# Other pacing for the second layer's image part beside the third and fourth tile of expert rows

## The chip, the cores and the metric

The kernel runs on one core of a Trainium2 chip. The metric is the device time of one execution in microseconds (us). Five engines work side by side: TensorE (PE, matrix products), VectorE (DVE), ScalarE (ACT), GpSimd (POOL, which here issues the gathers of expert rows) and SyncE (SP, which here issues the weight loads). They are tied together by semaphores only: an engine works through its own list in order, and an instruction that waits holds up everything behind it in that list.

## The reference, cut to what matters

Three layers of one network run one after another over 256 image tokens (x) and, in the first layer, 256 context tokens (ctx). Two layers are of the first kind, one is of a second kind. All is fp32, the model width is 1024. A layer of the first kind is a token mixer and then a retrieval over 16384 experts:

```
for l in range(DEPTH):                       # DEPTH = 2
    h  = _modulate(x,   norm1_g[l], m_x[0], m_x[1])
    hc = _modulate(ctx, norm1_g[l], m_c[0], m_c[1])
    mix_x, _ = _token_mix(h, lp, ang, kv_c)  # attention, Fourier mix, pooling, three sigmoid gates
    x = x + m_x[2] * mix_x
    h2 = _modulate(x, norm2_g[l], m_x[3], m_x[4])
    x = x + m_x[5] * _peer(h2, ...)
    if not last: the same for ctx

def _token_mix(h, lp, ang, kv_ctx):
    z = h @ lp["w_in"]
    cq, ckv, kr, zf, zp, zg = jnp.split(z, SPLITS, axis=-1)
    ...
    g = sigmoid(zg + lp["b_gate"])
    return (g_a * y_a + g_b * y_b + g_c * y_c) @ lp["w_out"], (k, v)

def _peer(...):   # for each token the 128 best experts (8 heads x 16)
    a   = einsum("tkd,td->tk", peer_down[ee], hh)
    act = gg * gelu(a)
    return einsum("tk,tkd->td", act, peer_up[ee])
```

With depth 2, the image part of the second layer's mixer (norm, projections `h @ w_in`, the attention vectors, Fourier and pooling mix, two of its three gated branches) needs the image tokens only, and these are finished when the first layer's experts of the two image tiles are done. The context tiles' experts still run then.

## The kernel before, in words

The tokens of the first layer form four tiles of 128: tiles 0 and 1 are x, tiles 2 and 3 are ctx. The expert stage (`gather`) goes through 4 x 128 = 512 rows; a row is the same place k of the 128 chosen experts for all 128 tokens of a tile. For row s, POOL fetches 128 vectors of `peer_down` (512 KB) and, for row s-18 (`LAG`), 128 vectors of `peer_up` (another 512 KB). DVE multiplies the down vectors with the token vectors and sums (a 128x1024 instruction, L1360). ACT applies the activation for 16 rows at a time and makes from each weight column a 128x128 diagonal matrix (L2809). PE multiplies the diagonal with the up vectors and adds into PSUM. In tiles 0 and 2 PE does both halves of the 1024 columns (L2150 and L2152); in tiles 1 and 3 PE does the first half alone and DVE the second half (L1387). An fp32 product is two instructions in the trace, so a row of the third tile is four 128x512 instructions on PE and a row of the fourth tile two. There are five buffers for down vectors and five for up vectors (`ND`, `NU`, L83): POOL fetches into one when the row that used it has been consumed (L3042 and `freed`, L3066).

Beside the rows runs other work, as a list of small units. `weave` (L216) sets the order on every engine. After each row the allowance `owed` grows by the rate (1.15 in this stage, `RATE0`), and as long as it is 1.0 or more one more unit is put behind the row, and its cost is taken off. `at` (L255) gives the units of a stage their cost; without it a unit costs 1.0. A unit that says `("after", n)` sets `hold`: no further unit is put in before row n. Each engine emits its own part of a unit at the same place of its own list.

The list beside the first layer's rows is `ctx_then_x` (L691): the queries of the image tiles, the whole context part of the first layer's mixer, the context tiles' queries and expert choice, and last `x_mix` (L671), the image part of the second layer's mixer. `x_mix` is, in order:

- `modulate`: norm and transposes of the image tokens, 6 units of cost 1.0
- `tok_major` twice (L1810 on PE): `h @ w_in` for 512 and then 416 columns, two units each; a unit is eight products of 128x512 or 128x416
- `qkvs` (L342): latent norms, query, key and value products, rotation, transposes, for two tiles, 12 units
- `spread` (L1929): Fourier and pooling mix, 9 units
- `gates` (L1971): for each of 8 column blocks of 128 a weight load by SP, then three gate products (eight products of 128x256 each) and two branch products (two of 128x256 each): 40 units

SP loads each weight block into one of two slots here, and a load waits until PE has read the slot's earlier content (L3082). After the 512 rows, 18 more steps finish the up vectors; then a fence ends the stage, and the image part's rest (`x_second`) follows on its own.

Of the kernel before, what the change touches and what calls it, by code (L numbers as in the profile page):

```python
# [85 lines left out]
NEXT = 128  # L86
# [47 lines left out]
class Walk:  # L134
# [447 lines left out]
    def main(self):  # L582

        K, A, NB = self.K, self.K.A, self.K.NB
        GR, BG, BCR, GR2 = K.GR, K.BG, K.BCR, K.GR2
        area = lambda *ranges: Mem(K.arena, *ranges)
        zrow = lambda t: K.H2[:, t, 0:928]
        zpair = lambda who: K.H2[:, 2 * who:2 * who + 2, 0:928]
        tables, gelu, gelu2 = (A["peer_down"], A["peer_up"]), ACT.Gelu_apprx_tanh, ACT.Gelu

        def temps(mem):
            return dict(qt=mem(768), kt=mem(768), kvt=mem(1024), junk=mem(256), rt=mem(3, 128), CQ=mem(2, 128), CK=mem(128))
# [11 lines left out]
        HTc, KTc, VVc = m0(8, 256), m0(8, 256), m0(2, 512)  # L604
        after_c = BG + 5120
        QT, AFP = m0(8, 256), m0(8, 256)
        AT, FT, PL = AFP[:, 0:4, :], AFP[:, 4:6, :], AFP[:, 6:8, :]
# [60 lines left out]
        MX, ga = K.arena[:, T0:T0 + 2048].rearrange("p (k n) -> p k n", n=256), K.arena[:, T0 + 2048:T0 + 4096].rearrange("p (k n) -> p k n", n=256)  # L668
        L1E = T0 + 4096

        def x_mix():  # L671
            yield ("after", 2 * NEXT + 6)
            self.modulate_rows(1, A["norm1_g"][1], 0, 0)
            yield ("after", 2 * NEXT + LAG + 2)
            self.folded(2)
            self.fence()
            yield from self.at(1.0, self.modulate(1, A["norm1_g"][1], 0, 0, HTc))
            self.fence()
            for c0, n in ((0, 512), (512, 416)):
                yield from self.at(1.8, self.tok_major(1, c0, n, lambda i: K.H2[:, i, c0:c0 + n], (HTc,)))  # L680
            self.fence()
            self.small_weights(1)
            tm = temps(area((T0, NB)))
            yield from self.at(1.4, self.qkvs(1, tm, [(t, zrow(t), QT, KTc, VVc) for t in (0, 1)]))
            self.fence()
            yield from self.spread(1, PL, FT, zpair(0), MX.rearrange("p (f c) n -> p f c n", c=2)[:, 0:2, :, :], MX[0:64, 4:8, :])
            self.fence()
            mem = area((L1E, NB))
            yield from self.at(1.6, self.gates(1, {1: FT, 2: PL}, MX, [mem(256) for _ in range(3)] + [ga], mem(256), HTc))

        def ctx_then_x(queries):  # L691
            yield from ctx_mix(queries)
            yield from x_mix()
# [2759 lines left out]
```

## Time and profile before

| | |
|---|---|
| median of 3 runs | 4397.4 us (4389.34 to 4398.44) |
| profiled execution | 4398.4 us, span 4396.6 us |
| PE busy | 3386.3 us, 77% |
| DVE busy | 2579.1 us, 59% |
| POOL busy | 2034.0 us, 46% |
| ACT busy | 815.1 us, 19% |
| moved by DMA | 1330.31 MB, mean 303 GB/s |

The page cuts the span into 40 slices of 110 us. In each line a digit is a share in tenths; `PEclk` is the clock that the chip granted TensorE, `DMA` the mean busy share of the 16 DMA engines. The first layer's expert rows run from about 452 us to 2072 us (slices 5 to 19), the second layer's from about 2300 us, the third's from about 3640 us. Between them the DMA engines rest while PE works alone. Two levels of the granted clock occur, 1.2 and 2.4 GHz; the tables show their mean over a stretch as a share of the higher one, so 0.50 is the lower level throughout.

### The profile page before, as it was taken

The page shows a single profiled execution, that of the slowest core. Times are in us where ns is not written, and L with a number is a line of the kernel's source. Part 1 is how long each engine was busy: PE and PEld are TensorE (multiplying, and loading weights), DVE is VectorE, ACT ScalarE, POOL GpSimd, SP SyncE. Part 2 cuts the span into 40 slices and gives each one's busy share as a digit, 9 for nine tenths or more (in the row PEclk, how much of TensorE's full clock was granted, in tenths as well). Part 3 has the DMA queues.
Part 4 walks back from the last instruction along what each step waited for, and adds up shares of the span by engine and source line. Part 5 has one row for each costly group of instructions (what it writes and reads, how often), then busy time and mean ns, then how long its engine had stood idle before and what let it go on. Part 6 is the DMA issues. An engine that isn't in the chain of part 4 may idle for free.

```text
span 4396.6 us, 35895 instructions
## 1 busy us (share of the span) xinstructions
PE 3386.3 (77%) x11238; PEld 1726.4 (39%) x11238; DVE 2579.1 (59%) x5454; ACT 815.1 (19%) x1924; POOL 2034.0 (46%) x2148
## 2 busy tenths in 40 slices
PE   6889786888768789866687866676878887876666
PEld 2357442455334246511254422221366654422111
DVE  1412767566776844776346674667563347684776
ACT  1311111222111121211221111111231111111111
POOL 0200566656555645666116665566100005676665
PEclk9999899999879899955898988775989998999556
DMA  6663998999999989999849999999500039999999
GB/s 226 227 239 131 343 372 317 365 371 409 400 363 340 343 307 367 402 368 370 303 155 358 341 358 405 357 404 379 181 1 1 1 112 343 342 350 368 373 372 340
DMA packets 380787, 1330.31 MB, mean 303 GB/s; under 512 B 39500, under 2 KB 44876, under 8 KB 377016
## 3 DMA queue, kind: packets, MB, share of 16 engines
q0 software_dynamic: 313344, 1141.10, 69.2%
q1 hardware_dynamic: 61104, 164.18, 10.1%
q10 hardware_dynamic: 6152, 22.74, 1.4%
q8 instruction: 93, 1.52, 0.1%
q14 instruction: 94, 0.77, 0.0%
HBM read 1326.69 MB, written 1.17 MB: 302 GB/s over the span
## 4 chain that ended last, share of the span: by engine, by line
PE 31%; DVE 21%; DMA 16%; issue 13%; POOL 12%; another core or an unknown queue 5%; ACT 3%; DVEq 0%; ACTq 0%; POOLq 0%
PE ps L1700 30%; POOL arena L3074 11%; DVE arena L905 7%; DMA arena<-in_peer_up,arena 7%; DVE arena L892 5%; DMA arena<-in_peer_down,arena 4%; ACT arena L2461 2%; DMA arena<-in_peer_u,arena 2%; PE ps L1706 1%; DVE arena L1297 1%; DVE arena L1286 1%; DVE arena L1281 1%; DVE arena L1276 1%; DVE arena L913 1%
## 5 line engine op out<-in xcount | busy, mean ns | idle before, releaser
L1700 PE MATMUL ps<-arena 128*128 128x512 f32 (+8 forms) x10500 | 3282.6, 493 | 870.5 <-DMA arena<-in_peer_up,arena 239.3
L1700 PEld LDWEIGHTS ps<-arena 128*128 128x128 f32 (+4 forms) x10500 | 1633.5, 198 | 2446.7 <-issue 1928.0
L905 DVE SCALAR_TENSOR_TENSOR arena<-arena,ps 128x1024 f32<-128x1024 f32 x1024 | 1238.8, 1216 | 541.7 <-DMA arena<-in_peer_down,arena 269.2
L3074 POOL DMA_INDIRECT arena<-in_peer_down,arena x768 | 744.1, 969 | 667.8 <-DVE arena L909 270.0
L3074 POOL DMA_INDIRECT arena<-in_peer_up,arena x768 | 734.4, 956 | 566.0 <-PE ps L1700 295.2
L2461 ACT ACTIVATE arena<-arena 128x128 f32<-128x128 f32 (+5 forms) x1242 | 446.3, 386 | 1945.7 <-PE ps L1700 586.8
L3074 POOL DMA_INDIRECT arena<-in_peer_u,arena x256 | 245.7, 960 | 645.2 <-DVE arena L909 537.8
L905 DVE SCALAR_TENSOR_TENSOR ps<-arena,ps 128x512 f32<-128x512 f32 x508 | 383.3, 754 | 136.2 <-DMA arena<-in_peer_up,arena 73.4
L2461 ACT ACTIVATE arena<-ps 128x512 f32<-128x512 f32 (+4 forms) x349 | 191.0, 547 | 1145.2 <-PE ps L1700 630.8
L3074 POOL DMA_INDIRECT arena<-in_peer_v,arena x256 | 243.6, 952 | 153.4 <-issue 69.7
L892 DVE TENSOR_TENSOR arena<-ps,arena 128x512 f32<-128x512 f32 (+3 forms) x192 | 131.2, 684 | 265.0 <-PE ps L1700 220.6
L892 DVE TENSOR_TENSOR arena<-arena 128x512 f32<-128x512 f32 (+8 forms) x398 | 246.7, 620 | 66.9 <-ACT arena L2461 41.3
L1706 PE MATMUL ps<-arena 128*128 128x128 f32 (+2 forms) x738 | 129.6, 314 | 133.7 <-DVE arena L892 69.5
L892 DVE TENSOR_TENSOR arena<-arena,ps 128x256 f32<-128x256 f32 (+1 forms) x134 | 73.0, 545 | 229.5 <-PE ps L1700 194.0
L1706 PEld LDWEIGHTS ps<-arena 128*128 128x128 f32 (+2 forms) x738 | 97.4, 157 | 216.6 <-issue 113.9
L909 DVE COPY arena<-ps 128x512 f32<-128x512 f32 (+5 forms) x69 | 39.6, 574 | 202.2 <-PE ps L1700 149.6
L2461 ACT ACTIVATE arena<-ps,arena 128x256 f32<-128x256 f32 (+2 forms) x140 | 71.0, 507 | 415.5 <-PE ps L1700 257.8
L2461 ACT ACT_TABLE_LOAD x79 | 101.4, 1283 | 64.5 <-DVE arena L892 29.7
L1276 DVE MAX8 arena<-ps 128x8 f32<-128x128 f32 x128 | 28.6, 287 | 133.6 <-PE ps L1700 70.4
L3020 POOL DMA_DIRECT2D arena<-in_w_mod x40 | 30.5, 763 | 133.3 <-PE ps L1700 70.5
L905 DVE DVE_READ_ACCUMULATOR arena<-arena,ps 128x1 f32 x1024 | 84.2, 82 | 0.0
L913 DVE TENSOR_REDUCE arena<-ps 128x1 f32<-128x512 f32 (+2 forms) x50 | 30.3, 606 | 73.1 <-PE ps L1700 65.6
(34 smaller groups left out, 560.5 us busy)
## 6 DMA issues: line engine op xcount, KB each, us to landing
arena<-in_w_mod POOLq DMA_DIRECT2D x40, 1024.0 KB, 6.5
arena<-in_gate_blocks SPq DMA_DIRECT2D x16, 2048.0 KB, 7.8
arena<-in_w_in SPq DMA_DIRECT2D x14, 2048.0 KB, 7.8
arena<-in_w_pq SPq DMA_DIRECT2D x13, 2048.0 KB, 16.0
arena<-in_ada_w POOLq DMA_DIRECT2D x24, 1024.0 KB, 7.9
arena<-in_w_out SPq DMA_DIRECT2D x8, 2048.0 KB, 8.0
arena<-in_gate_blocks SPq DMA_DIRECT2D x8, 1792.0 KB
arena<-mod_scratch ACTq DMA_DIRECT2D x26, 512.0 KB
```

Source lines behind the costliest of these rows:

```text
L892: self.e.tensor_tensor(o, a, b, op).then_inc(*(inc or self.inc(self.S.vec)))
L905: self.e.scalar_tensor_tensor(o, a, s, b, op0, op1, accum_out=accum).then_inc(*(inc or self.inc(self.S.vec)))
L909: self.e.tensor_copy(o, a).then_inc(*(inc or self.inc(self.S.vec)))
L913: self.e.tensor_reduce(o, a, AX, op).then_inc(*(inc or self.inc(self.S.vec)))
L1276: e.max(v[j][:, 0:8], src[j]).then_inc(*self.inc(S.vec))
L1281: e.max_index(ix[j][:, 0:8], v[j][:, 0:8], src[j]).then_inc(*self.inc(S.vec))
L1286: e.match_replace(tmp[j], v[j][:, 0:8], src[j], NEG).then_inc(*self.inc(S.vec))
L1297: e.max_index(ix[j][:, 8:16], v[j][:, 8:16], tmp[j]).then_inc(*(self.drain(b) if last else self.inc(S.vec)))
L1700: return self.e.matmul(o, l, r, start=start, stop=stop)
L1706: ins = self.e.transpose(o, x, self.K.ident)
L2461: self.e.activation(o, i, f, bias=bias, scale=scale, accum_out=accum).then_inc(*(inc or self.inc(self.S.act)))
L3074: self.e.indirect_dma_start(out=o, out_offset=None, in_=table, in_offset=bass.IndirectOffsetOnAxis(ap=idx.bitcast(U32), axis=0)).then_inc( ...
```

## The change

Four numbers in the list beside the rows. The two projection stages cost 6.0 a unit where they cost 1.8, `qkvs` costs 2.8 where it cost 1.4, `spread` costs 2.8 where it cost 1.0, and a hold at row 384 (3 x `NEXT`) is put ahead of the gates, whose own cost stays 1.6. No instruction of the computation is added or removed.

```diff
             for c0, n in ((0, 512), (512, 416)):
-                yield from self.at(1.8, self.tok_major(1, c0, n, lambda i: K.H2[:, i, c0:c0 + n], (HTc,)))
+                yield from self.at(6.0, self.tok_major(1, c0, n, lambda i: K.H2[:, i, c0:c0 + n], (HTc,)))
             self.fence()
             self.small_weights(1)
             tm = temps(area((T0, NB)))
-            yield from self.at(1.4, self.qkvs(1, tm, [(t, zrow(t), QT, KTc, VVc) for t in (0, 1)]))
+            yield from self.at(2.8, self.qkvs(1, tm, [(t, zrow(t), QT, KTc, VVc) for t in (0, 1)]))
             self.fence()
-            yield from self.spread(1, PL, FT, zpair(0), MX.rearrange("p (f c) n -> p f c n", c=2)[:, 0:2, :, :], MX[0:64, 4:8, :])
+            yield from self.at(2.8, self.spread(1, PL, FT, zpair(0), MX.rearrange("p (f c) n -> p f c n", c=2)[:, 0:2, :, :], MX[0:64, 4:8, :]))
             self.fence()
+            yield ("after", 3 * NEXT)
             mem = area((L1E, NB))
             yield from self.at(1.6, self.gates(1, {1: FT, 2: PL}, MX, [mem(256) for _ in range(3)] + [ga], mem(256), HTc))
```

PE's list at the second projection block, before. The 128x416 products are this block's two units, the 128x128 transposes begin `qkvs`; the 128x512 products between them are up products of the third tile, two to a row, save eight in the first group that are the first block's last unit.

```order
L1700 MATMUL ps<-arena 128x512 x24
L1700 MATMUL ps<-arena 128x416 x8
L1700 MATMUL ps<-arena 128x512 x2
L1700 MATMUL ps<-arena 128x416 x8
L1700 MATMUL ps<-arena 128x512 x4
L1706 MATMUL ps<-arena 128x128 x2
L1700 MATMUL ps<-arena 128x512 x2
L1706 MATMUL ps<-arena 128x128
```

The same place of the changed kernel (its lines from 688 on are one higher):

```order
L1701 MATMUL ps<-arena 128x512 x38
L1701 MATMUL ps<-arena 128x416 x8
L1701 MATMUL ps<-arena 128x512 x10
L1701 MATMUL ps<-arena 128x416 x8
L1701 MATMUL ps<-arena 128x512 x10
L1707 MATMUL ps<-arena 128x128 x2
L1701 MATMUL ps<-arena 128x512 x6
L1707 MATMUL ps<-arena 128x128
```

Between two projection units stood one row's up products and now stand five rows'; between two units of `qkvs` stood one row's and now two or three.

PE's list where the gates begin, before: eight 128x256 are a gate product, two are a branch product.

```order
L1700 MATMUL ps<-arena 64x256 x2
L1700 MATMUL ps<-arena 128x512 x2
L1700 MATMUL ps<-arena 64x256 x4
L1700 MATMUL ps<-arena 128x512 x2
L1700 MATMUL ps<-arena 128x256 x8
L1700 MATMUL ps<-arena 128x512 x2
L1700 MATMUL ps<-arena 128x256 x8
L1700 MATMUL ps<-arena 128x512 x4
L1700 MATMUL ps<-arena 128x256 x2
```

And now:

```order
L1701 MATMUL ps<-arena 64x256 x2
L1701 MATMUL ps<-arena 128x512 x2
L1701 MATMUL ps<-arena 64x256 x4
L1701 MATMUL ps<-arena 128x512 x3
L1701 MATMUL ps<-arena 128x256 x8
L1701 MATMUL ps<-arena 128x512 x2
L1701 MATMUL ps<-arena 128x256 x8
L1701 MATMUL ps<-arena 128x512
L1701 MATMUL ps<-arena 128x256 x2
```

The gates moved from rows of the third tile (two 128x512 products each) to rows of the fourth (one each): where one row or two lay between two units, that was two or four products and is now one or two.

## Rows read from the trace of the kernel before

**Rows 1.** The page's slices: granted clock, DMA share, GB/s.

```profile
PEclk9999899999879899955898988775989998999556
DMA  6663998999999989999849999999500039999999
GB/s 226 227 239 131 343 372 317 365 371 409 400 363 340 343 307 367 402 368 370 303 155 358 341 358 405 357 404 379 181 1 1 1 112 343 342 350 368 373 372 340
```

**Rows 2.** Windows of the first layer's last rows, all engines.

```profile
core 0: us, PE busy (x) PEld busy (x) DVE busy (x) ACT busy (x) POOL busy (x), PEclk, DMA share, GB/s
1519.00:1561.00 42.00, 29.91 (x69) 13.13 (x68) 25.39 (x46) 12.11 (x27) 21.60 (x23) 0.82 0.92 339
1561.00:1605.00 44.00, 40.66 (x105) 19.10 (x105) 13.95 (x31) 10.04 (x27) 17.81 (x19) 1.00 0.79 278
1605.00:1640.00 35.00, 29.84 (x95) 14.59 (x94) 25.44 (x64) 9.47 (x25) 20.40 (x22) 0.95 0.93 325
1640.00:1704.00 64.00, 62.52 (x215) 37.69 (x214) 22.75 (x45) 16.07 (x38) 32.25 (x35) 1.00 0.91 334
1704.00:1849.00 145.00, 135.41 (x488) 90.80 (x486) 90.23 (x155) 31.95 (x78) 86.29 (x92) 1.00 1.01 399
1849.00:2072.00 223.00, 155.79 (x159) 38.74 (x160) 158.37 (x245) 32.65 (x85) 147.12 (x158) 0.54 0.98 372
```

**Rows 3.** The same windows for DVE's row instructions alone (line L905).

```profile
core 0: us, DVE busy (x), PEclk, DMA share, GB/s
1519.00:1561.00 42.00, 18.45 (x28) 0.82 0.92 339
1561.00:1605.00 44.00, 9.66 (x17) 1.00 0.79 278
1605.00:1640.00 35.00, 14.24 (x23) 0.95 0.93 325
1640.00:1704.00 64.00, 18.88 (x34) 1.00 0.91 334
1704.00:1849.00 145.00, 78.75 (x126) 1.00 1.01 399
1849.00:2072.00 223.00, 158.06 (x240) 0.54 0.98 372
```

**Rows 4.** Chain that ended last, 1555 to 1710 us, its longest pieces: start, us.

```profile
1554.95 32.28 PE ps L1700 x81
1596.46 7.76 PE ps L1700 x20
1618.74 11.18 PE ps L1700 x28
1637.46 25.79 PE ps L1700 x83
1666.96 19.40 PE ps L1700 x68
1687.19 23.15 PE ps L1700 x81
```

**Rows 5.** Timeline of DVE, then POOL: start, us, instruction, idle before it.

```profile
1579.94 0.59 DVE L909 COPY arena<-ps 128x416 f32<-128x416 f32 x1 [15.25 <-PE ps L1700]
1572.85 0.94 POOL L3074 DMA_INDIRECT arena<-in_peer_up,arena  x1 [5.65 <-PE ps L1700]
```

**Rows 6.** Timeline of PE: a third-tile row, and one projection block with rows.

```profile
1615.34 1.89 PE L1700 MATMUL ps<-arena 128*128 128x512 f32 x4
1560.81 29.84 PE L1700 MATMUL ps<-arena 128*128 128x512 f32 x75
```

**Rows 7.** Groups by shape, 1561 to 1849 us: xcount, busy us, mean ns, idle before.

```profile
L1700 PE MATMUL ps<-arena 128*128 128x256 f32 x480 | 111.3, 379 | 1.4 <-DVE arena L921 1.4
L2461 ACT ACT_TABLE_LOAD x11 | 14.1, 1283 | 9.6 <-PE ps L1700 8.8
L1700 PE MATMUL ps<-arena 128*128 128x416 f32 x32 | 11.5, 512 | 0.0
L1700 PE MATMUL ps<-arena 128*128 128x384 f32 x16 | 5.5, 485 | 0.0
L1706 PE MATMUL ps<-arena 128*96 128x128 f32 x32 | 4.6, 288 | 3.6 <-issue 3.6
```

**Rows 8.** Groups by shape, 1849 to 2072 us, rows with nothing beside them.

```profile
L1700 PE MATMUL ps<-arena 128*128 128x512 f32 x159 | 156.6, 1086 | 67.7 <-DMA arena<-in_peer_up,arena 41.1 <-issue 25.4 <-ACT arena L2461 1.2
L905 DVE SCALAR_TENSOR_TENSOR arena<-arena,ps 128x1024 f32<-128x1024 f32 x80 | 97.7, 1221 | 53.2 <-DMA arena<-in_peer_down,arena 34.1 <-issue 19.1
```

**Rows 9.** All of the first layer's rows: DVE line L905, one window.

```profile
453.00:2072.00 1619.00, 797.83 (x1273) 0.87 0.97 364
```

**Rows 10.** The page's DMA issues: the second layer's gate blocks, KB each.

```profile
arena<-in_gate_blocks SPq DMA_DIRECT2D x8, 1792.0 KB
```

## The prediction, made before the changed kernel had run

> **What bounds the kernel now.** I read the page's slices first [rows 1]. Where expert rows run the DMA digit is nearly always 9 (90% or more), so how fast 1 MB a row comes in sets the time. It dips to 8 in the fifteenth slice, 1539 to 1649 us, which is where the diff works. So I cut that part into windows [rows 2] and counted rows in each by DVE's own row instructions [rows 3]: two for a row of the third tile (the product and the read of its sum), three for one of the fourth.
>
> From 1849 to 2072 us the rows have nothing beside them: 240/3 = 80 rows in 223 us, 2.79 us a row, DMA share 0.98, 372 GB/s, and both PE and DVE wait mostly for the gathers [rows 8]. That is the DMA's pace. From 1561 to 1605 us there are 17/2 = 8.5 rows in 44 us, 5.2 us a row; DMA share 0.79, PE busy 40.66 of 44 at full clock. From 1605 to 1640: 11.5 rows, 3.0 each, DMA 0.93. From 1640 to 1704: 17 rows, 3.8 each, DMA 0.91, PE busy 62.52 of 64. From 1704 to 1849: the third tile's last 18 rows of down products take 36 of the 126 instructions and the other 90 are 30 rows, so 48 rows, 3.02 each, DMA 1.01 at 399 GB/s. In all 8.5+11.5+17+48+80 = 165 rows in 511 us.
>
> The chain says what the slow windows wait for [rows 4]: one piece of 32.28 us on PE, then 25.79, 19.40 and 23.15, with little between. Meanwhile DVE sits 15.25 us before one copy of a projection's result, with row products queued behind it, and POOL sits 5.65 us until PE frees an up buffer [rows 5]. So PE is the bound there, and the DMA engines lose 0.21 x 44 + 0.07 x 35 + 0.09 x 64 = 9.2 + 2.5 + 5.8 = 17.5 us.
>
> **Where the units stand now.** Counting the allowance through the list (1.15 a row), the preceding work ends at row 341 in both kernels, norm at 342 to 346, the first projection unit at 347. Before, the other three stand at 349, 351, 352; `qkvs` at 354 to 367; `spread` 368 to 376; gates 376 to 430; rows 431 to 530 are bare. Now the projections stand at 347, 353, 358, 363; `qkvs` 368 to 395; `spread` 397 to 417; gates 420 to 475; rows 476 to 530 are bare. The hold at 384 decides nothing, because the new costs reach row 417 first. All fits before the last row, so nothing is pushed behind the stage; the last row is still about 37 + 18 steps away.
>
> **The sum.** PE's needs at full clock: a third-tile row 1.89 us standing alone and 4 x 0.40 = 1.6 in a dense run (29.84 us for 75 instructions) [rows 6], I count 1.89; a projection unit 16 x 29.84/75 = 6.4 us [rows 6] or 11.5/2 = 5.8 [rows 7]; the whole of `qkvs` about 5.5 + 4.6 [rows 7] + eight 128x512 at 0.40 = 3.2 + small transposes, 15 us; gates 448 of the 480 instructions of 128x256, 448/480 x 111.3 = 104 us [rows 7]. A fourth-tile row is half of 1.89, 0.95.
>
> 1. Rows 348 to 368 (20, with three projection units): PE 20 x 1.89 + 18 = 56 us, 2.8 a row; DMA wants 2.79. Both near the limit and in lumps: a unit of 6 us behind one row and none behind the next four. Bounds: 2.8, and 3.95, the 79 us of 1561 to 1640 us over its 20 rows. I take 3.2, since the nearest window with units as thin beside third-tile rows ran at 3.0 [rows 2, 3] and the lumps come on top: 64 us.
> 2. Rows 368 to 401 (33, `qkvs` at half its density and two units of `spread`): PE 62 + 16 = 78 us, 2.4 a row. Bounds 2.79 and 3.4 (window of 1519 to 1561 us has 14 rows in 42 us = 3.0; the stage as a whole, 1619 us for 512 rows [rows 9], 3.16; PE at a mean clock of 0.7 would give 3.4). The window at twice the density of `qkvs` made 3.0, but it began with filled buffers, so I take 3.1: 102 us.
> 3. Rows 401 to 420 (19 light rows with `spread`): 2.8 to 3.1, taken 2.9: 55 us.
> 4. Rows 420 to 475 (55, all gates): PE 55 x 0.95 + 104 = 156 us, 2.84 a row. DMA: 55 x 1.049 MB plus eight blocks of 1.835 MB, of which one or two come in early (a slot is free after row 363, the other after `spread`), 57.7 + 12 = 69.7 MB [rows 10] at the 399 GB/s of the window that carries such blocks [rows 2]: 175 us, 3.2 a row. The gates were DMA-bound there before and stay so.
> 5. Rows 475 to 512 (37 bare) at 2.79: 103 us.
>
> Sum 64 + 102 + 55 + 175 + 103 = 499 against 511 us: 12 us less. Checks from outside: the bytes of 1561 to 2072 us are 44 x 278 + 35 x 325 + 64 x 334 + 145 x 399 + 223 x 372 = 186 MB. With 70 MB of it at 399 and the rest at 372 GB/s that is 175 + 312 = 487 us, so 24 us is all that this change can give back, and I expect half.
>
> Small edits on the way. ACT gets two more table loads, 81 against 79 in its list, because the activation of 16 rows falls between more of the square roots: 2 x 1.28 us [rows 7] on an engine busy 48 of 143 us from 1561 to 1704 and less beyond [rows 2]; hidden, at worst 2.6 us. The fences are the same in number and stand between units as before. SP's loads wait for slots that free later in rows; the first gate blocks still come before their products. The takeover of the token vectors at row 384 makes DVE wait for ACT; it now falls among `qkvs` units where it fell among gate units; either way ACT waits for PE there, and less if PE is not behind. After the stage nothing has moved.
>
> The profiled execution took 4398.4 us, 1.8 us beyond its span; 4398.4 - 12 = 4386.4 us. It lies 1.0 us above the median of the runs shown, within their 9 us spread. Forecast: 4386 us.
>
> **The rivals.**
>
> A. *Handovers, not PE's load, cost the time.* Every `qkvs` unit sends a value through ACT, DVE, PE and back while rows queue behind each wait. If spreading them only spreads the waits, rows 348 to 420 run at the stage's mean of 3.16 [rows 9]: 228 us where the forecast has 221, and up to 5 more if the 20 rows at the projections take 3.4. That leaves 0 to 5 us of the 12: about 4395, no change that can be told. For it: the fast part of the slow stretch still had DMA 0.93. Against it: the chain is PE by far [rows 4].
>
> B. *All of the DMA's idle time comes back.* 487 us by the bytes: 4374 us. Against it: no window with work beside third-tile rows reached 0.98 before.
>
> C. *PE's clock falls in the third tile, and the kernel gets slower.* Before, dense work kept the clock at 1.00 from 1561 to 1849 us; in the bare rows it is 0.54, and at 1519 to 1561, PE busy 30 of 42 us, it was 0.82 [rows 2]. Thinner work leaves PE pauses. A product instruction takes 1.086 us at the low level [rows 8], so a third-tile row 4.3 us. If the mean clock over rows 348 to 401 is 0.72, PE needs (56 + 78)/0.72 = 186 us there, where the forecast has 166, and pays waits of some 5 us on top: 4386 + 24 = 4410 us, slower by 12. It decides from a mean clock of about 0.78 down (172 us, and the waits, eat the 12 us gained). [...]
>
> The Trainium skill speaks for this rival: the page "TensorE: Matmul & The Clock Gate", section "HAM oscillation — how this bites in real kernels", advises to keep products together ahead of a DMA wait so that PE stays warm, the opposite of this change. The trace agrees that bare rows run at the low level; by that rule the time would be C's, by the rows the forecast's.
>
> D. *The change does not do what it says.* The gates do not begin with the fourth tile's first row but 36 rows later. That costs nothing by the count above, since 55 bare steps remain.
>
> **How the numbers follow.** I hold a change within 0.2% (9 us) for not told from none. Forecast, a gain of 6 to 18 us: 0.52. A: 0.24. B: 0.11. C: 0.13. D changes no time and has no chance of its own. Faster by more than 9 us: three quarters of the forecast's case and B, 0.39 + 0.11 = 0.50. Within 9 us: the rest of it and A, 0.13 + 0.24 = 0.37. Slower by more than 9 us: C, 0.13. The range runs from B's 4374 to 4402, which takes in A and the lighter cases of C and leaves under 2 in 10 out.
>
> **What would show it.** In the changed kernel's windows: row 348 to 368 should show a DMA share of 0.90 or more where 0.79 stood, and no DVE wait of 15 us before a projection copy. The clock over rows 348 to 401 should stay above 0.85. Gates should run at 3.2 us a row with a DMA share of 1.0, then about 37 bare rows at 2.8. The stage's last down product should come 12 us earlier. Wrong would be: clock below 0.78 (C); clock high, PE idle and still 3.2 us a row (A); gate rows above 3.3 us, which would mean that I sized the weight traffic too small.

## The result and the profile after

The changed kernel took 4367.35 us (median of 4 runs, 4356.71 to 4372.49) against 4393.37 us for the kernel before on the same chip: ratio 0.9926, 95% interval 0.9905 to 0.9947. It is faster by 26 us, where 12 were forecast and 4374 us was the lower end of the range. In a later comparison, of 7 runs against 27, the ratio was 0.9958, interval 0.9941 to 0.9975, which is 18 us. The two intervals overlap, so no closer number than 18 to 26 us can be given. The profiled execution took 4364.67 us, its span 4362.9 us.

The page's slices after, in the form of [rows 1]:

```profile
PEclk9999899999979899996899988866988998999556
DMA  6663998999999999999849999999400039999999
GB/s 228 227 237 130 338 363 320 375 356 409 401 362 355 343 378 352 392 410 375 298 159 369 333 365 392 372 405 374 157 1 1 1 113 338 352 350 372 379 369 346
```

The digit of the fifteenth slice, 8 before, is 9, and the rate of that slice is 378 GB/s where it was 307. Now the windows. The kernel after is cut where rows 336, 348, 368, 401, 420, 475 begin and row 511 ends, as DVE's row products show them (its lines from 688 on are one higher). First all engines, then DVE's row instructions alone:

```profile
core 0: us, PE busy (x) PEld busy (x) DVE busy (x) ACT busy (x) POOL busy (x), PEclk, DMA share, GB/s
1518.00:1552.00 34.00, 23.98 (x56) 10.05 (x55) 24.78 (x44) 12.43 (x28) 22.81 (x23) 0.82 0.99 375
1552.00:1617.00 65.00, 61.60 (x149) 27.84 (x148) 27.07 (x50) 14.18 (x33) 38.85 (x42) 0.99 0.93 363
1617.00:1720.00 103.00, 84.64 (x223) 39.33 (x221) 53.49 (x116) 24.50 (x64) 64.51 (x69) 0.94 0.96 364
1720.00:1775.00 55.00, 32.70 (x70) 13.09 (x71) 40.21 (x69) 8.93 (x25) 32.85 (x35) 0.79 0.96 362
1775.00:1946.00 171.00, 154.81 (x559) 104.29 (x558) 115.08 (x192) 36.82 (x91) 104.89 (x113) 0.99 1.02 405
1946.00:2043.00 97.00, 67.40 (x71) 16.73 (x70) 72.18 (x113) 15.50 (x38) 63.82 (x69) 0.57 0.99 378
```

```profile
1552.00:1617.00 65.00, 24.97 (x43) 0.99 0.93 363
1617.00:1720.00 103.00, 39.07 (x66) 0.94 0.96 364
```

The stretch from row 336 to the end of row 511, which the windows of both kernels cover from nearly the same microsecond (1518.9 and 1518.2), is the measure used below. It holds the same work in all kernels here, save where an edit below takes work out, adds some or moves other work into it. Before, its first profile and a second one (`before_again`), then after, first and second (`after_again`):

```profile
1519.00:2071.00 552.00, 453.66 (x1123) 213.63 (x1121) 335.18 (x580) 111.79 (x277) 324.77 (x347) 0.80 0.96 361
```

```profile
1523.00:2073.00 550.00, 455.28 (x1122) 214.21 (x1121) 335.04 (x579) 111.86 (x277) 324.34 (x347) 0.79 0.96 362
```

```profile
1518.00:2043.00 525.00, 425.12 (x1123) 211.33 (x1121) 332.81 (x580) 112.36 (x279) 327.73 (x347) 0.87 0.98 380
```

```profile
1527.00:2057.00 530.00, 430.85 (x1123) 215.82 (x1121) 330.87 (x580) 111.87 (x280) 328.54 (x348) 0.85 0.98 377
```

To a tenth: 552.5 and 550.8 us before, 525.1 and 530.2 after. The stretch lost 24 us on the mean of the two, 27.4 in the first pair; the rest of the first pair's 33.7 us lies in stages that the change does not touch. The bytes are the same, 552 x 361 and 525 x 380 GB/s are both 199 MB: the gain is the rate. Part of it is idle time of the DMA engines, 0.96 of 552 busy against 0.98 of 525. The other part is that the packets themselves took less: share x 16 engines / rate is the time that one engine spent on a KB, 0.96 x 16 / 361 = 42.5 ns before and 0.98 x 16 / 380 = 41.3 ns after.

The waits of [rows 5] are gone from the projections. DVE copies the first result of each projection block, and ACT the second. DVE's two copies after, in its timeline, with no idle time noted before either:

```profile
1558.62 0.69 DVE L910 COPY arena<-ps 128x512 f32<-128x512 f32 x1
1595.14 0.59 DVE L910 COPY arena<-ps 128x416 f32<-128x416 f32 x1
```

### The profile page after: what moved, and what is told of

It reads as the page before. It is cut to its first block, busy times and chain, and to the rows that moved or that the text cites. A ratio compares the mean times of both kernels' runs of the same rounds, so it can differ in the third digit from the quotient of the medians.

```text
span 4362.9 us, 35889 instructions
## 1 busy us (share of the span) xinstructions
PE 3358.4 (77%) x11238; PEld 1715.0 (39%) x11238; DVE 2577.2 (59%) x5454; ACT 816.5 (19%) x1926; POOL 2040.9 (47%) x2148
## 4 chain that ended last, share of the span: by engine, by line
PE 15%; DVE 10%; DMA 9%; issue 7%; POOL 5%; another core or an unknown queue 3%; ACT 2%; ACTq 0%; DVEq 0%; POOLq 0%
PE ps L1701 15%; POOL arena L3075 5%; DMA arena<-in_peer_up,arena 5%; DVE arena L893 3%; DVE arena L906 3%; DMA arena<-in_peer_v,arena 2%; ACT arena L2462 1%; DMA arena<-in_ada_w 1%; DMA arena<-in_peer_u,arena 1%; DMA arena<-in_peer_down,arena 1%; PE ps L1707 1%; DVE arena L914 1%; DVE arena L1287 1%; DVE arena L1282 0%
## 5 line engine op out<-in xcount | busy, mean ns | idle before, releaser
L1701 PE MATMUL ps<-arena 128*128 128x512 f32 (+9 forms) x10500 | 3254.6, 490 | 873.9 <-ACT arena L2462 231.9
L893 DVE TENSOR_TENSOR arena<-arena 128x512 f32<-128x512 f32 (+8 forms) x398 | 246.9, 620 | 72.1 <-ACT arena L2462 42.1
L893 DVE TENSOR_TENSOR arena<-arena,ps 128x256 f32<-128x256 f32 (+1 forms) x134 | 73.0, 545 | 222.7 <-PE ps L1701 171.2
```

Source lines behind the costliest of these rows:

```text
L893: self.e.tensor_tensor(o, a, b, op).then_inc(*(inc or self.inc(self.S.vec)))
L1701: return self.e.matmul(o, l, r, start=start, stop=stop)
```

## The experiments

All stretches are from row 336 to the end of row 511. "Row 368" is the time from row 336 to row 368: 121.1 and 119.9 us before, 98.5 and 99.8 after. In each fence of windows the first row is rows 336 to 368 and the second the whole stretch, rounded to whole microseconds.

**proj_only: the first number alone.**

```diff
-                yield from self.at(1.8, self.tok_major(
+                yield from self.at(6.0, self.tok_major(
```

> Only the first of the four numbers: the projection units cost 6.0, everything else as before. By the allowance the projections stand at rows 347 to 363 as in the changed kernel, the attention vectors at 368 to 382, spread to 390, gates 391 to 445, so most gates also leave the third tile. Measure: time from row 336 to the end of row 511, 552.5 us before and 525.1 us in the changed kernel. Theory P (PE's load beside third-tile rows is the bound, and any thinning gives back the DMA's idle time there): 24 to 28 us of the 27 come from here, because by row 368 the changed kernel is already 22.6 us ahead; stretch 525 to 529 us, device time 22 to 28 us under before. Theory H (handovers of the attention vectors cost, and their pacing matters as much): the dense attention vectors at rows 368 to 382 lose what they lost before, some 8 to 10 us; stretch 534 to 537 us.

```profile
1512.00:1610.00 98.00, 85.37 (x203) 38.37 (x202) 51.71 (x94) 25.35 (x61) 58.76 (x63) 0.91 0.94 362
1512.00:2046.00 534.00, 442.78 (x1123) 213.18 (x1122) 335.39 (x581) 113.68 (x280) 326.79 (x348) 0.82 0.97 374
```

534.2 us; device time ratio 0.9968 (0.9951 to 0.9984). All of the lead at row 368 is there (98.8), but 4 to 6 us of it are lost again by row 384 (158.3 against 152.0 and 154.6). The projections' pacing brings 17 to 18 us, most of the gain though not all of it. The number lies at the edge of H's range, and its loss stands where H put it: rows 368 to 401, with the attention vectors still dense, took 113.1 us where the changed kernel took 103.8 and 104.3. What of these last 4 to 9 us is handovers and what is PE's load, this run does not tell.

**vectors_only: the second and third number alone.**

```diff
-            yield from self.at(1.4, self.qkvs(
+            yield from self.at(2.8, self.qkvs(
-            yield from self.spread(1, PL, ...
+            yield from self.at(2.8, self.spread(1, PL, ...
```

> Only the second and third number: attention vectors and spread at 2.8, projections dense as before. Attention vectors at rows 354 to 380, spread to 402, gates 405 to 459. Theory P: the dense projections still cost their 14 to 20 us (rows 344 to 360), the rest is given back because the gates have left the third tile; stretch 540 to 543 us, device time 9 to 13 us under before. Theory H: the handovers were the loss, so most of it comes back; stretch 528 to 533 us.

```profile
1515.00:1625.00 110.00, 91.50 (x223) 41.37 (x222) 55.97 (x110) 27.08 (x71) 55.73 (x60) 0.90 0.88 323
1515.00:2053.00 538.00, 432.81 (x1122) 211.35 (x1120) 333.86 (x580) 109.74 (x278) 325.04 (x347) 0.85 0.97 371
```

538.1 us; ratio 0.9981 (0.9966 to 0.9995). Row 352 is where it was before (63.0 against 62.7), so the dense projections still cost; after them it gains 14 us, 11 of them by row 368 (110.5). P said 540 to 543, because the gates leave the third tile, and missed by 2 us; most of the gain stands where the attention vectors were thinned, and `gates_late` shows that the gates' move alone brings none. By the stretch the two parts alone make 31 to 33 us together, where both at once brought 24 to 27; by the device times they make 14 and 8 us, which is no more than the 18 to 26 of both. So whether they give back partly the same idle time is not shown.

**gates_late: old costs, the gates held to row 402.**

```diff
+            yield ("after", 3 * NEXT + LAG)
             mem = area((L1E, NB))
```

> Old costs throughout, but the gates held until row 402, the first whose up products DVE shares. Projections, attention vectors and spread dense at rows 347 to 376 as before, nothing beside rows 377 to 401, gates 402 to 451. Theory P: this removes the PE-bound gates beside third-tile rows (DMA idle 5.8 us from 1640 to 1704 us) and nothing of the projections'; stretch 544 to 548 us, 4 to 8 us under before. Theory G (that the gates beside third-tile rows were the main cost): 535 us or less. If the weight traffic alone were what counts, no change: 550 to 554 us.

```profile
1514.00:1635.00 121.00, 99.16 (x265) 46.37 (x264) 64.60 (x139) 31.64 (x79) 60.69 (x64) 0.92 0.87 311
1514.00:2066.00 552.00, 439.54 (x1124) 211.75 (x1123) 333.26 (x582) 109.51 (x277) 328.45 (x348) 0.85 0.95 362
```

551.7 us, no change; ratio 0.9993 (0.9975 to 1.0011). At row 384 it was 16 us ahead (169.6 against 185.2), and by row 475 all was gone (448.6 and 449.2). Rows 401 to 420 and 420 to 475 of this kernel, then of the kernel before:

```profile
1741.00:1804.00 63.00, 56.61 (x206) 40.02 (x204) 40.75 (x72) 12.28 (x30) 33.27 (x36) 0.95 0.92 350
1804.00:1963.00 159.00, 126.83 (x356) 68.60 (x356) 112.06 (x184) 29.54 (x76) 101.22 (x108) 0.85 1.01 394
```

```profile
1755.00:1817.00 62.00, 55.22 (x206) 38.14 (x206) 41.02 (x70) 15.77 (x36) 36.98 (x40) 1.00 1.01 397
1817.00:1968.00 151.00, 112.93 (x192) 40.06 (x190) 111.11 (x174) 24.51 (x64) 99.59 (x108) 0.65 0.99 382
```

The gates' 15 MB of weights had not come yet and came later, while the DMA share fell to 0.92 where the first gates met the change of tiles. So it is not the gates leaving the third tile that pays. P, which gave 544 to 548 us, missed here as G did; the number is that of the third case, no change. Why that share fell is open.

**thin_proj: the schedule of before, a quarter of the projections' products** (so later values differ from the reference).

```diff
+            ks = (0, 7) if l == 1 and n > 400 else range(8)
-            for k in range(8):
+            for k in ks:
```

> The kernel before with its schedule unchanged, but each projection unit of the second layer's image part does two of its eight products (the contraction is cut to a quarter, so the later values are not the reference's); loads, evictions, fences and all waits stay. It takes 24 of the 32 products, 18.6 us of PE at full clock, out of rows 347 to 352. Theory P: PE's load is the bound there, so the stretch shortens by 14 to 19 us, to 534 to 539 us. Theory H (the waits between engines bound it): less than 5 us, 548 us or more.

```profile
1517.00:1620.00 103.00, 82.54 (x220) 37.97 (x220) 65.81 (x141) 31.87 (x80) 62.00 (x64) 0.91 0.98 369
1517.00:2049.00 532.00, 432.81 (x1075) 203.96 (x1074) 335.76 (x581) 111.54 (x278) 327.31 (x347) 0.80 0.98 375
```

531.5 us, 19 to 21 less than before and 2.5 beyond P's range; ratio 0.9953 (0.9934 to 0.9971). All waits between engines stand where they stood in the lists, and taking 18.6 us of products out wins 18 to 19 us by row 368 (102.2). H, which gave less than 5 us, falls. The loss at the projections is PE's load.

**before_again and after_again** are the two kernels unchanged.

> The kernel before once more, to see how far the stretch from row 336 to the end of row 511 repeats from profile to profile. It was 552.5 us; the single-edit kernels that share its first rows agree within 0.5 us up to row 352 (62.7, 62.9, 63.0), so I expect 550 to 555 us.

> The changed kernel once more: stretch 523 to 528 us (525.1 before), and a tighter ratio of the device times; from the stretch alone 27 us or 0.6% are expected.

550.8 and 530.2 us. The second is 2 us outside its range: the stretch of the changed kernel repeats only to about 5 us, and differences smaller than that between the kernels below are none.

**gates_thin: the gates thinner still.**

```diff
-            yield from self.at(1.6, self.gates(1,
+            yield from self.at(2.2, self.gates(1,
```

> The changed kernel with the gates at 2.2 instead of 1.6 a unit, so that they fill rows 420 to 495 instead of 420 to 475 and 16 bare rows are left before row 512 instead of 37. Theory M (rows with weight loads among them move 400 to 410 GB/s, bare rows 365 to 377, because the DMA engines have more to choose from): rows 430 to 512 take 94 MB / 0.41 = 229 us where they took 236.8; stretch 517 to 521 us. Theory N (the mix does not matter, the bytes are only moved about): no change, 523 to 528 us.

```profile
1511.00:1613.00 102.00, 85.81 (x203) 37.99 (x202) 51.40 (x93) 26.55 (x61) 60.34 (x64) 0.92 0.93 355
1511.00:2039.00 528.00, 416.89 (x1123) 214.06 (x1121) 332.41 (x580) 112.79 (x281) 323.94 (x345) 0.89 0.98 378
```

528.2 us: theory M falls. Rows 430 to 512 took 241.2 us where M gave 229, and 236.8 and 240.3 in the changed kernel. Stretching the weight loads over more rows wins nothing. Ratio to before 0.9957 (0.9939 to 0.9975), that of `after_again` beside it 0.9958.

**warm_pe: PE kept busy in the bare rows of the kernel before.**

```diff
                 self.wait_ge(*there)
                 ...
+                if len(tiles) == 4 and s >= 440:
+                    spare = K.psum[:, 3584:4096]
+                    self.wait_ge(S.free[7], self.uses[7])
+                    self.mm(spare, K.ident, K.H2[:, 3, 0:512], True, True)
+                    self.mm(spare[:, 0:256], K.ident, K.H2[:, 3, 0:256], True, True)
```

> The kernel before, with two products whose result nobody reads (128x512 and 128x256, identity as weights) added on PE ahead of each row's up product from row 440 on, where rows are bare. [...] Theory W (bare rows are slow because PE at the low level frees the up buffers 1 us later): rows 448 to 512 fall from 2.84 to about 2.6 us each, 15 us in all. Theory M (the DMA's own rate for a lone queue is the bound): no change in those rows, within 3 us. Theory L (the added load itself counts): slower by the amount that PE goes over the row, seen as PE busy near 1.

Rows 448 to 512 of this kernel, then of the kernel before:

```profile
1890.00:2072.00 182.00, 153.15 (x384) 67.94 (x382) 126.45 (x195) 23.25 (x66) 117.75 (x126) 0.99 0.97 367
```

```profile
1890.00:2071.00 181.00, 126.09 (x127) 30.92 (x126) 125.67 (x194) 26.16 (x68) 118.79 (x128) 0.53 0.98 364
```

The clock went from 0.53 to 0.99 and the rows did not get faster. That does not yet make them the DMA's alone, because the run did not do what theory W needs, to free the up buffers earlier. The added products stand behind the wait for the up vectors (`there`), ahead of the row's own product. Here is one row of this kernel, with six instructions, and one of the kernel before, with two:

```profile
1951.28 2.39 PE L1700 MATMUL ps<-arena 128*128 128x512 f32 x6 [0.17 <-DMA arena<-in_peer_up,arena]
1903.63 2.04 PE L1700 MATMUL ps<-arena 128*128 128x512 f32 x2 [0.50 <-DMA arena<-in_peer_up,arena]
```

From the landing of the vectors to the free buffer PE took 2.4 us where it took 2.0, so what the clock gave the added work took away. W stays open by this run. Rows 440 to 448 moved 347 GB/s with the products added, where the two profiles before show 404 and 378. The kernel as a whole is slower, ratio 1.0033 (1.0017 to 1.0049), and the added products also stand in the 18 steps after the last down row: from the end of row 511 to the next stage's first row it took 240.3 us where before took 231.7, which is 9 of the 13 us between the medians.

**copy_late: DVE's copy one unit later, PE's list as before.**

```diff
+        late = l == 1 and n > 400
         for i in range(2 * len(HTs)):
             b = self.bank()
-            yield
-            if i % 2 == 0:
+            if late and i == 1:
+                yield
+                self.wait_ge(*self.full(first))
+                self.copy(dst(0), first.ap[:, 0:n], inc=self.drain(first))
+                continue
+            first = b
+            yield
+            if i % 2 == 0 and not late:
```

> The kernel before, with one thing moved: DVE's copy of a projection's first result stands one unit later in DVE's list for the second layer's image part (two rows further on). PE's list is the same. Theory P (PE's load beside third-tile rows): DVE's wait moves elsewhere, POOL still waits for PE to free up buffers, and by row 368 nothing is won: 119 to 121 us from row 336, stretch 549 to 553 us. Theory C (the copy that holds DVE's rows costs by itself): by row 348 it stands at 35 us as in the changed kernel, where the kernel before stands at 41 to 42, and by row 368 it is 6 us or more ahead; stretch 542 to 546 us.

POOL's waits for PE at the projections in this kernel:

```profile
1560.25 0.94 POOL L3081 DMA_INDIRECT arena<-in_peer_up,arena  x1 [6.74 <-PE ps L1707]
1570.57 0.94 POOL L3081 DMA_INDIRECT arena<-in_peer_up,arena  x1 [5.64 <-PE ps L1707]
```

551.4 us; ratio 0.9986 (0.9967 to 1.0004). By row 348 it stood at 35.2, 6 us ahead as theory C has it; by row 356 all but 1 us of that was gone, and at row 368 it had 119.6. POOL waited 5.64 us for PE where [rows 5] have 5.65. The 15.25 us that DVE sat before the copy were no cost of their own: had it not waited there, it would have waited for rows.

**proj_34: the changed kernel, projections at 3.4.**

```diff
-                yield from self.at(6.0, self.tok_major(
+                yield from self.at(3.4, self.tok_major(
```

> The changed kernel with the projections at 3.4 a unit instead of 6.0, so at rows 347, 350, 353 and 356, three up rows between two units where there were one or two before and are five now; the rest follows at the new pace, gates at 411 to 465. Theory P: three rows and a unit want 3 x 1.6 to 1.9 + 6.4 = 11 to 12 us of PE, 3.8 a row, still over the 2.6 to 2.8 of the DMA, but the debt is paid over the thin rows that follow, and five down and five up buffers cover little of it; row 368 at 103 to 108 us from row 336 (98.5 to 99.8 in the changed kernel, 120 to 121 before), stretch 529 to 534 us. If only the leaving of the dense place counted, it would stand at 99.

```profile
1527.00:1635.00 108.00, 92.94 (x220) 41.35 (x219) 54.98 (x103) 25.71 (x65) 60.04 (x62) 0.91 0.91 339
1527.00:2060.00 533.00, 434.35 (x1124) 214.58 (x1122) 334.70 (x580) 112.16 (x279) 327.86 (x346) 0.85 0.98 374
```

533.0 us and 107.2 at row 368, as PE's load has it: three rows' room for a unit gives about two thirds of the lead at row 368, five rows' room all. Ratio 0.9939 (0.9920 to 0.9958), not to be told from the changed kernel's.

**norm_thin and ctx_thin: the same idea one stage earlier, and beside the first tile.**

```diff
-            yield from self.at(1.0, self.modulate(1, ...
+            yield from self.at(2.6, self.modulate(1, ...
```

> The changed kernel with the norm's six units at 2.6 instead of 1.0, one per 2.3 rows; everything behind moves by eight rows, gates end at row 483. In the changed kernel rows 344 to 352 still show a DMA share of 0.79. Theory P: the four units of transposes (0.6 us each on PE) and the DVE products of the norm (1.2 to 1.3 us, five of them) come as a lump; thinned, 2 to 4 us come back, stretch 522 to 526 us against 525.1 and 530.2. Rival: the loss there is the chain of the norm itself (square, mean, root), which spacing does not shorten: no change, 525 to 531 us.

```diff
-            yield from self.at(1.4, self.qkvs(0, ...
+            yield from self.at(2.2, self.qkvs(0, ...
-            yield from self.at(0.97, self.attend(2, ...
+            yield from self.at(1.15, self.attend(2, ...
```

> The changed kernel with the same idea applied to the first layer's context part, beside the first tile's rows (PE does both halves of the up products there too): attention vectors at 2.2 instead of 1.4 and attention at 1.15 instead of 0.97 a unit; all that follows moves ten rows on, the gates of the second layer end at row 485. Rows 96 to 144 ran at a DMA share of 0.85 to 1.0 and 307 to 393 GB/s. Theory P: 4 to 8 us come back there, measured from row 96 to row 224, and the stretch from 336 is not comparable since other work stands in it; device time 4 to 8 us under the changed kernel's. Rival: these rows wait for the softmax's handovers (row maximum on DVE, exponential on ACT), not for PE's load, and spacing wins less than 3 us.

norm_thin stood at 195.0 us at row 401, 7 to 9 ahead of the changed kernel, and ended at 528.3, level with it and outside P's 522 to 526. ctx_thin took 418.7 us from row 96 to row 224 where the changed kernel took 427.6 and 434.5 and the kernel before 427.2 and 427.6. The 13 other profiles, which hold the same work in these rows, lie between 423.4 and 434.7, so some 5 us are won there. Its row 511 ended at 2052.0 us of the span where the changed kernel's ended at 2043.3 and 2056.9: won early, not there at the end. Ratios 0.9916 (0.9888 to 0.9943) and 0.9926 (0.9898 to 0.9953), of four runs each. Both intervals overlap those of the changed kernel, so no version here is shown to beat it.

## Why the prediction was wrong, step by step

The mechanism was right: PE was the bound beside the third tile's rows (`thin_proj`), thinning gave the DMA engines most of their idle time there back, and the clock stayed high (0.99 and 0.94, not under 0.78), so rival C did not come. The size was off, and two terms of the sum did it. Rows 336 to 348, which the sum left out as unchanged, gave 6 to 8 us, and the last 37 rows, put at 103 us, took 97 and 96. Together they are the 12 us that the forecast lacked. The terms of the sum, with both profiles of the changed kernel:

| rows | forecast | after, after_again | before, before_again |
|---|---|---|---|
| 336 to 348 | not in the sum | 34.2, 35.4 | 42.3, 41.0 |
| 348 to 368 | 64 | 64.3, 64.4 | 78.8, 78.9 |
| 368 to 401 | 102 | 103.8, 104.3 | 114.6, 114.2 |
| 401 to 420 | 55 | 54.7, 54.7 | 62.4, 62.4 |
| 420 to 475 | 175 | 171.2, 175.6 | 151.1, 150.9 |
| 475 to 512 | 103 | 96.9, 95.8 | 103.3, 103.4 |

1. *The sum began at row 348.* The forecast held everything before as unchanged, since the first unit stands at row 347 in both kernels. But the copy of its result stands in DVE's list at the next unit's place, two rows on before and six now, and DVE's rows queue behind it. The window lost 6 to 8 us. `copy_late` and `proj_only` both show 35 us there, and so does `thin_proj` (35.3), where the copy stands at its old place but PE's unit before it is short. By itself the later copy is worth nothing, as `copy_late` shows; together with PE's relief it stays.
2. *Bare rows at 2.79 us.* The last 37 rows took 2.6 each. The mean of 2.79 came from a window of 80 rows [rows 3] and was applied to a piece of 37 right behind the gates. In both kernels the first 18 rows behind the last gate ran faster than the others, and only then fell back to 2.7 to 2.9 us each: before, rows 430 to 448 took 46.2 us, 2.57 each; after, rows 475 to 493 took 45.2 and 42.1 us, 2.5 and 2.3 each. In the short piece they weigh twice as much: 6 to 7 us. These rows and the bare ones that follow, before, then after, then `after_again`:

```profile
1843.00:1890.00 47.00, 34.31 (x47) 9.73 (x45) 37.17 (x59) 9.52 (x24) 31.28 (x34) 0.67 1.02 406
1890.00:1968.00 78.00, 54.52 (x55) 13.31 (x54) 53.35 (x83) 11.33 (x30) 51.27 (x56) 0.52 0.97 359
1946.00:1991.00 45.00, 31.54 (x34) 8.11 (x34) 35.37 (x57) 8.02 (x19) 30.48 (x33) 0.58 0.99 383
1991.00:2043.00 52.00, 35.86 (x38) 8.62 (x36) 36.81 (x57) 7.47 (x19) 33.34 (x37) 0.57 0.98 373
1961.00:2003.00 42.00, 31.85 (x33) 7.81 (x32) 34.95 (x56) 7.38 (x18) 29.14 (x31) 0.54 1.02 405
2003.00:2057.00 54.00, 35.76 (x38) 8.62 (x36) 37.04 (x57) 7.86 (x21) 35.02 (x38) 0.56 0.95 354
```

3. *Gate rows*, 175: 171 and 176, right within what repeats, with a DMA share of 1.02. The projections and attention vectors came within 3 us of their terms, so the steps of 3.2 and 3.1 us a row held. Rows 348 to 420 ran at 3.1, near rival A's 3.16; the gain that A missed lay before and behind them.
4. *"I expect half."* The outer check by the bytes gave 487 us for rows 348 to 512, "all that this change can give back", a gain of 24, and rival B got 0.11. Measured were 490.9 and 494.8 us, so B's count was not reached there: beside third-tile rows the share rose to 0.93 and 0.96, not to 0.98. That the whole stretch gained 24 us, and the device time 26, then 18 us, is B's number by another sum, since 6 to 8 us of it lie before row 348, where B counts nothing. Still, half of the ceiling had no reason behind it. The one given against B, that no window had reached a share of 0.98 beside third-tile work, named the effect as its own proof: in those windows PE's load held the share down, and it was PE's load that was being taken away. `thin_proj` shows a share of 0.98 in rows 336 to 368 once the projections are light.
5. *17.5 us of idle time by the share.* The share undercounts the loss, because the packets of the slow windows also took longer (0.87 x 16 / 313 = 44.5 ns per KB in rows 336 to 368 before, 0.95 x 16 / 367 = 41.4 after). Bytes over rate counts both. Why they took longer is open.
6. *ACT busy 48 of 143 us.* From 1561 to 1704 us the windows of [rows 2] sum to 36 us; the 48 takes in the window before. It only strengthens the point made with it.

Of the signs named beforehand the DMA share and the clock beside the third tile, the copies and the gate rows came as said; the bare rows at 2.8 did not, and the last down product came 28 and 16 us earlier in the span, not 12. Rival D was right in its facts, the gates began at row 420, and without a price, as said.

## What to carry to other kernels

Where a stream of transfers should set the pace, reckon a change by bytes over the best rate the same mix reached, not by the idle share; when the thing that held the rate down is taken away, start from that rate and subtract only for what has a measured reason. Start the sum where the first engine's list differs, not where the first moved unit stands. Take the pace of a short piece from rows at the same place behind the same work, not from the mean of a long one. Pace work beside such a stream by the room that its bound engine has left in each row: here a unit of 6.4 us had enough with five rows with about 1 us to spare each, and three rows gave part of the gain; nothing between was run. With the stream at a share of 0.98, thinning more or elsewhere (`gates_thin`, `norm_thin`, `ctx_thin`) moved the loss about and won nothing that could be told, and a wait seen on an engine that is not the bound (15 us of DVE here) is no cost until the bound one is relieved.

## What the runs showed of the hardware

For the 18 rows behind the last gate the gathers alone moved 406 GB/s before (394 in `before_again`) and 383 and 405 after. Then they moved 359 before (366), and 373 and 354 after. The granted clock does not tell the two paces apart: it was 0.54 where `after_again` moved 405 GB/s and 0.56 where it moved 354. What ends the faster stretch is open. Whether bare rows would be faster if PE freed the up buffers earlier was not tested: `warm_pe` had the clock at 0.99 where it was 0.53, but freed them later, and took 182 us where before took 181.

A DMA engine spent 40 to 46 ns on a KB, reckoned from share and rate of a window, weight loads included: 1.02 x 16 / 405 = 40.3 in the gate rows after, 0.79 x 16 / 278 = 45.5 in the slowest window before. The share alone does not set it, since two windows with a share of 0.93 gave 45.8 (325 GB/s, before) and 41.0 (363 GB/s, after).
